# A mixer and mixture-of-experts block: gates applied where expert rows leave PSUM, and another division of the last sums

## The reference, cut to what matters

```python
h2 = rms_norm(x, norm2_g[layer]) * (1 + sc2) + sh2
f = moe_ffn(tokens, router_w, router_b, moe_w1[layer], moe_w3[layer], moe_w2[layer])
#   in moe_ffn, for each expert e:
#   he = jax.nn.silu(h @ w1[e]) * (h @ w3[e])
#   y = y + gates[:, e:e + 1] * (he @ w2[e])
x = x + g2 * f
return rms_norm(x, final_g)
```

## Time and profile before

| | us |
|---|---|
| median of three runs | 611.53 |
| the profiled execution, whole | 612.55 |
| its span, first to last instruction | 610.8 |
| TensorE busy | 546.6 (89%) |
| VectorE busy | 454.0 (74%) |
| ScalarE busy | 319.2 (52%) |
| GpSimd busy | 120.7 (20%) |

### The profile page before, as it was taken

One profiled execution on the slowest core, in us unless ns is written; L12 is line 12 of the kernel. 1 busy time (PEld: TensorE's weight loads), 2 busy tenths in 40 slices (PEclk: granted clock), 3 DMA queues, 4 the chain that ended last, 5 costly groups with the idle time before them and its releaser, 6 DMA issues.

```text
span 610.8 us, 7418 instructions
## 1 busy us (share of the span) xinstructions
PE 546.6 (89%) x2657; PEld 409.5 (67%) x2657; DVE 454.0 (74%) x580; ACT 319.2 (52%) x392; POOL 120.7 (20%) x123
## 2 busy tenths in 40 slices
PE   2889988999999999966999999999999999999860
PEld 2446843677676788733578788888888887877640
DVE  1358695545586545349779999999999999998687
ACT  4531141345425912254357688667768766767214
POOL 5001915333310600025211111001111101100510
PEclk9799998999999999986999999999999999999985
DMA  8999997268214700167789999999999999997543
GB/s 308 389 372 318 380 329 258 86 200 302 70 69 171 243 35 39 66 246 276 241 303 392 379 392 386 393 391 393 391 391 390 387 387 389 363 390 234 182 162 137
DMA packets 88809, 171.50 MB, mean 281 GB/s; under 512 B 5513, under 2 KB 18509, under 8 KB 88785
## 3 DMA queue, kind: packets, MB, share of 16 engines
q1 hardware_dynamic: 82498, 152.81, 70.1%
q10 hardware_dynamic: 2768, 9.97, 4.0%
q0 software_dynamic: 3520, 8.42, 3.8%
HBM read 158.58 MB, written 16.79 MB: 287 GB/s over the span
## 4 chain that ended last, share of the span: by engine, by line
PE 67%; DMA 14%; DVE 8%; ACT 4%; SPq 3%; issue 3%; POOL 0%; DVEq 0%; ACTq 0%; POOLq 0%
DMA ada<-in_ada_w 9%; PE psum L1195 4%; PE psum L1222 4%; PE psum L1197 4%; PE psum L1196 4%; PE psum L1224 4%; PE psum L1223 4%; PE psum L1207 3%; PE psum L1206 3%; PE psum L1205 3%; PE psum L920 3%; DMA w<-in_moe_w 3%; PE psum L922 3%; PE psum L921 3%; PE psum L1057 2%
## 5 line engine op out<-in xcount | busy, mean ns | idle before, releaser
L2058 DVE TENSOR_TENSOR w_lo<-w,w_hi 128x2048 fp32r<-128x2048 f32 x32 | 73.0, 2285 | 2.6 <-ACT w_hi L1574 2.6
L2047 DVE TENSOR_TENSOR w_lo<-w,w_hi 128x1024 fp32r<-128x1024 f32 (+2 forms) x30 | 68.4, 2282 | 0.0
L1574 ACT CAST w_hi<-w 128x2048 fp32r<-128x2048 f32 x32 | 60.4, 1919 | 10.8 <-DMA w<-in_moe_w 5.4
L1565 ACT CAST w_hi<-w 128x2048 fp32r<-128x2048 f32 x30 | 57.2, 1910 | 14.4 <-PE psum L1207 12.0
L2041 DVE TENSOR_TENSOR w_lo<-w,w_hi_a 128x2048 fp32r<-128x2048 f32 (+1 forms) x30 | 51.6, 1758 | 4.7 <-ACT w_hi_a L1561 4.7
L762 POOL COPY idx<-idx 128x1 int32 x14 | 12.6, 903 | 194.7 <-PE psum L1169 184.2
L1222 PE MATMUL psum<-w_hi,heT_hi 128*128 128x512 f32 x120 | 49.7, 414 | 0.8 <-DVE w_lo L2058 0.8
L1740 DVE SCALAR_TENSOR_TENSOR rows<-ada,cc,rows 128x512 f32<-128x512 f32 x48 | 41.6, 871 | 9.1 <-DMA ada<-in_ada_w 7.6
L1224 PE MATMUL psum<-w_hi,heT_lo 128*128 128x512 f32 x120 | 47.0, 392 | 0.0
L1196 PE MATMUL psum<-w_lo,xgT_hi 128*128 128x512 f32 x120 | 46.7, 389 | 0.0
L1223 PE MATMUL psum<-w_lo,heT_hi 128*128 128x512 f32 x120 | 46.7, 389 | 0.0
(11 more groups left out here) (338 smaller groups left out, 1214.3 us busy)
## 6 DMA issues: line engine op xcount, KB each, us to landing
w<-in_moe_w SPq DMA_DIRECT2D x32, 2048.0 KB, 13.8
w<-in_moe_w SPq DMA_DIRECT2D x32, 1024.0 KB, 13.8
ada<-in_ada_w SPq DMA_DIRECT2D x12, 2048.0 KB, 18.1
win<-in_w_in SPq DMA_DIRECT2D x8, 1024.0 KB, 14.5
expert_rows<-ysb ACTq DMA_DIRECT2D x15, 512.0 KB, 6.3
expert_rows<-zero SPq DMA_DIRECT2D x1, 4608.0 KB, 18.4
wout<-in_w_out SPq DMA_DIRECT2D x4, 1024.0 KB, 5.0
x<-in_x SPq DMA_DIRECT2D x2, 1024.0 KB, 9.6
```

The costliest lines, as they stand in the source:

```text
L1574: act.copy(w2_hi[:, :, hs], w2_sb[b][:, :, hs]).then_inc(w2_hi_ok[half], 1)
L2047: v.tensor_tensor(w3_lo[b][:, ks, :], w3_sb[b][:, ks, :], w3_hi[:, ks, :], ALU.subtract).then_inc(w3_lo_ok, n)
L2058: v.tensor_tensor(w2_lo[b][:, :, hs], w2_sb[b][:, :, hs], w2_hi[:, :, hs], ALU.subtract).then_inc(w2_lo_ok[half], 1)
```

## The change

Gates move to the eviction. The router's gate is worked out before the overflow blocks, set out by slot through the same one-hot product (24 more columns, so that product goes from bf16 with 16 columns to fp32 with 40), copied to `gslot`, and for each block GpSimd copies one column to `gs1[b]`, which `expert_rows` takes as a scalar. The rows in DRAM then carry their gate; the sums at the end are plain additions. A row of the last block is now gathered from a spare block of zeros, for which the DRAM tensor and its zero fill grow by one block. The two gathered rows of tile 3 are no longer added by VectorE: TensorE multiplies them by the identity (plain fp32, two products for each half) into the banks in which the one-hot products accumulate, and waits for the last gather before all of them. For tiles 0 and 1 ScalarE writes x times the reciprocal (after the root of tile 1 and of tile 2), GpSimd multiplies by `final_g`, and SyncE's stores wait for that. `low_hidden` for the last block stands ahead of `add_rows(0)`.

```diff
-            gp.wait_ge(idx_ok, 2)
+            def next_gate(b, s):
+                gp.wait_ge(y1_copied, s - 1)
+                gp.sem_inc(gather_go, 1)
+                gp.tensor_copy(gs1[b][:], gslot[:, bass.ds(s, 1)]).then_inc(gs_ok, 1)
+            gp.wait_ge(idx_ok, 3)
+            for b in range(2):
+                gp.tensor_copy(gs1[b][:], gslot[:, b:b + 1]).then_inc(gs_ok, 1)
...
-            with gp.Fori(1, n_pairs) as i:
+            for b in range(2):
+                gather(b, 2 + b)
+            with gp.Fori(2, n_pairs) as i:
                 for b in range(2):
                     gather(b, i * 2 + b)
+                    next_gate(b, i * 2 + b - 2)
...
+            gp.wait_ge(gain_in, 48)
+            for t in range(2):
+                gp.wait_ge(scale_ok, 4 + t)
+                gp.tensor_tensor(ygat[:, t, 1, :], ygat[:, t, 1, :], fing[:], ALU.mult).then_inc(res_gp, 1)
...
-                    m = pe.matmul(bank[6][:, 0:2 * OVER], hot_slot[:, i, :],
-                                  hot_more[:, i].rearrange("p a b -> p (a b)"), start=(i == 0), stop=(i == 2 * NT - 1))
+                    m = pe.matmul(bank[6][:, 0:2 * OVER + NB], hot_mod[:, i, :], hot_more[:, i, :],
+                                  start=(i == 0), stop=(i == 2 * NT - 1))
...
-            pe.wait_ge(hot_last_ok, 1)
+            pe.wait_ge(hot_ok, 4)
+            pe.wait_ge(gat_in[NT - 1], 32)
             for half in range(2):
                 hs = slice(half * 512, (half + 1) * 512)
                 pe.wait_ge((y0_copied, y1_copied)[half], last + 1)
+                for k in range(2):
+                    pe.matmul(tok_bank(NT - 1, half)[:], ident[:], ygat[:, NT - 1, k, hs], start=(k == 0), stop=False)
...
+            def scaled(t):
+                act.wait_ge(rec_ok, t + 1)
+                act.activation(ygat[:, t, 1, :], x1[:, t, :], ACT.Copy, scale=st2[:, t, 7:8]).then_inc(scale_ok, 1)
...
+                if 1 <= t <= 2:
+                    scaled(t - 1)
...
-                v.tensor_tensor(ysb[b][:, cs_], bank[5 + half], rows[:, G2, cs_], ALU.mult
-                                ).then_inc((y0_copied, y1_copied)[half], 1)
+                v.scalar_tensor_tensor(out=ysb[b][:, cs_], in0=bank[5 + half], scalar=gs1[b][:, 0:1],
+                                       in1=rows[:, G2, cs_], op0=ALU.mult, op1=ALU.mult
+                                       ).then_inc((y0_copied, y1_copied)[half], 1)
...
-                    link(v.scalar_tensor_tensor(out=x1[:, t, :], in0=ygat[:, t, k, :], scalar=gate[:, t, k:k + 1],
-                                                in1=x1[:, t, :], op0=ALU.mult, op1=ALU.add))
+                    link(v.tensor_tensor(x1[:, t, :], ygat[:, t, k, :], x1[:, t, :], ALU.add))
...
             gated(last)
+            low_hidden(1, last)
             add_rows(0)
-            low_hidden(1, last)
+            expert_rows(1, last, final, 0)
             add_rows(1)
-            expert_rows(1, last, final, 0)
             low_last(0)
             expert_rows(1, last, None, 1)
+            add_rows(2)
             low_last(1)
-            add_rows(2)
-            add_last(0, 0)
-            add_last(1, 0)
+            v.wait_ge(gain_in, 48)
+            for t in range(3):
+                add_last(t, 0)
             add_last(0, 1)
             add_last(1, 1)
-            add_last(2, 0)
+            add_last(3, 0)
+            result(0)
             add_last(2, 1)
-            v.wait_ge(gain_in, 32)
-            result(0)
-            add_rows(3)
             result(1)
-            add_last(3, 0)
             add_last(3, 1)
             result(2)
             result(3)
```

More of the change, by code:

```diff
@@ L166, in build @@
         xgT_0 = at("xgT_0", 180 * K1, [P, KD, P])
+        hot_mod = at("hot_mod", 176 * K1, [P, NT * 2, P])
+        hot_more = at("hot_more", 198 * K1, [P, NT * 2, 2 * OVER + NB])
         xn = at("xn", 184 * K1, [P, NT, D])
@@ L192, in build @@
         iota_slot = at("iota_slot", cursor[1], [P, P], BF16)
-        in_last = at("in_last", cursor[1] + 256, [P, NT, 2])
-        gate_last = at("gate_last", cursor[1] + 288, [P, NT, 2])
+        gslot = at("gslot", cursor[1] + 352, [P, NB])
+        gs1 = [at(f"gs1_{b}", cursor[1] + 448 + 32 * b, [P, 1]) for b in range(2)]
         idx_last = at("idx_last", cursor[1] + 320, [P, 1])
@@ L247, in build @@
         wsel = rt("wsel", [P, NT, 2])
+        gate = rt("gate", [P, NT, 2])
+        in_last = rt("in_last", [P, NT, 2])
+        spare = rt("spare", [P, 1])
         den = rt("den", [P, NT, 1])
-        hot_blk = rt("hot_blk", [P, NT * 2, OVER])
+        hot_blk = rt("hot_blk", [P, NT * 2, NB])
         hot_base = rt("hot_base", [P, NT * 2, 2, NE], BF16)
-        hot_more = rt("hot_more", [P, NT * 2, 2, OVER], BF16)
         idx_f = rt("idx_f", [P, NB])
@@ L549, in _ @@
             sp.dma_start(y_dram[(NE - 1) * P:, :].rearrange("(p b) (q n) -> p (b q) n", p=P, n=256),
-                         zero[:].unsqueeze(1).to_broadcast([P, (OVER + 1) * 4, 256])).then_inc(stored, 16)
+                         zero[:].unsqueeze(1).to_broadcast([P, (OVER + 2) * 4, 256])).then_inc(stored, 16)
             for i in range(4):
@@ L629, in _ @@
                     cs_ = slice(half * 512, (half + 1) * 512)
-                    sp.wait_ge(res_ok, 2 * t + half + 1)
+                    sp.wait_ge(*((res_gp, t + 1) if t < 2 else (res_ok, 2 * t + half - 3)))
                     sp.dma_start(out_v[:, t, cs_], ygat[:, t, 1, cs_]).then_inc(stored, 16)
@@ L1296, in _ @@
                 pe.wait_ge((y0_copied, y1_copied)[half], last + 1)
+                for k in range(2):
+                    pe.matmul(tok_bank(NT - 1, half)[:], ident[:], ygat[:, NT - 1, k, hs], start=(k == 0), stop=False)
                 pe.wait_ge(ylast_hi_ok, half + 1)
                 for t in range(NT):
-                    pe.matmul(tok_bank(t, half)[:], last_hot[:, t * P:(t + 1) * P], y_hi[:, hs], start=True, stop=False)
+                    pe.matmul(tok_bank(t, half)[:], last_hot[:, t * P:(t + 1) * P], y_hi[:, hs],
+                              start=(t < NT - 1), stop=False)
                 pe.wait_ge(ylast_lo_ok, half + 1)
@@ L1729, in _ @@
             m.then_inc(hc_ok, 1)
[L1731 removed]
+            v.wait_ge(gain_in, 16)
             def mod_row(n):
@@ L2014, in overflow_blocks @@
                                        op0=ALU.mult, op1=ALU.add).then_inc(rmod_ok, 1)
+                pick(wsel[:], prob[:].unsqueeze(2).to_broadcast(E2))
+                link(v.tensor_tensor(den[:], wsel[:, :, 0:1], wsel[:, :, 1:2], ALU.add))
+                link(v.reciprocal(den[:], den[:]))
+                link(v.tensor_tensor(gate[:], wsel[:], wide(den[:], [P, NT, 2]), ALU.mult))
                 above(cs[:, 0, 8:], bank[7][:, NT * NE:(NT + 1) * NE], [P + 1, 2 * P + 1, 3 * P + 1])
@@ L2029, in overflow_blocks @@
                 link(v.tensor_tensor(blk_no[:], blk_no[:], off2[:], ALU.add))
-                fb = [P, NT * 2, OVER]
-                link(v.tensor_tensor(hot_blk[:], iota_blk[:, NE:NB].unsqueeze(1).to_broadcast(fb),
+                fb = [P, NT * 2, NB]
+                link(v.tensor_tensor(hot_blk[:], iota_blk[:].unsqueeze(1).to_broadcast(fb),
                                      blk_no[:].rearrange("p t k -> p (t k)").unsqueeze(2).to_broadcast(fb), ALU.is_equal))
-                v.tensor_scalar(hot_more[:, :, 0, :], hot_blk[:], tok[:, 0:1], None, ALU.mult)
-                v.tensor_tensor(hot_more[:, :, 1, :], hot_blk[:], tok_chunk[:].unsqueeze(2).to_broadcast(fb), ALU.mult
+                v.tensor_scalar(hot_more[:, :, 0:OVER], hot_blk[:, :, NE:], tok[:, 0:1], None, ALU.mult)
+                v.tensor_tensor(hot_more[:, :, OVER:2 * OVER], hot_blk[:, :, NE:],
+                                tok_chunk[:].unsqueeze(2).to_broadcast([P, NT * 2, OVER]), ALU.mult)
+                v.tensor_tensor(hot_more[:, :, 2 * OVER:], hot_blk[:],
+                                gate[:].rearrange("p t k -> p (t k)").unsqueeze(2).to_broadcast(fb), ALU.mult
                                 ).then_inc(hot_ok, 1)
@@ L2104, in overflow_list @@
                 v.tensor_scalar(blk_last[:], more[:], 2.0, float(NE - 1), ALU.mult, ALU.add)
+                v.tensor_scalar(spare[:], more[:], -2.0, float(NB - NE + 1), ALU.mult, ALU.add)
                 link(v.tensor_copy(ovf[:, 8:9], more[0:1, :]))
@@ L2110, in combine_terms @@
                 link(v.tensor_scalar(in_last[:], blk_no[:], blk_last[:, 0:1], None, ALU.is_equal))
-                link(v.tensor_tensor(blk_first[:], in_last[:], blk_no[:], ALU.mult))
-                link(v.tensor_tensor(blk_first[:], blk_no[:], blk_first[:], ALU.subtract))
+                link(v.scalar_tensor_tensor(out=blk_first[:], in0=in_last[:], scalar=spare[:, 0:1], in1=blk_no[:],
+                                            op0=ALU.mult, op1=ALU.add))
                 link(v.scalar_tensor_tensor(out=slot[:], in0=blk_first[:], scalar=float(P), in1=rmod[:],
@@ L2127, in _ @@
             overflow_list()
```

(4 more changed lines are left out.)

33 lines of the change are left out of this document (15 added, 18 removed).

## The result

The changed kernel takes 616.42 us (median of six runs, 613.23 to 621.12) against 610.82 for the kernel before on the same chips: 1.0094 of it, interval 1.0049 to 1.0140. Measured again beside other experiments it was 1.0079 (1.0054 to 1.0103), 615.71 against 610.87, which is +4.8 us. The profiled execution took 616.43 us, its span 614.7.

What follows compares the result with a forecast made beforehand. It took the end to be VectorE's, fed by gathers, and the blocks TensorE's. +1.7 at the start, +1.4 to the first whole tile and +1.0 behind it gave +4.1: 615.6 us against the median, range 610.3 to 617.6.

Steps and rivals of the forecast that it cites:

- The start: Index product before the expert blocks: fp32 passes on TensorE's path, 1.9 us less 0.21, +1.7; bounds 0 and 2.3.
- The loop: Expert blocks: longer evictions and GpSimd's gate copies are hidden and cost nothing; evictions 1.6 us in all if not.
- Rival 4: Expert blocks: gate copies too late for evictions, VectorE waits 0.5 us in 16 blocks, adding 8: 623.6 us; chance 0.03.
- To the first whole tile: End, up to the first finished tile: wait for the last gather, then sums at slow clock; tile whole at 596.6, +1.4.
- The last gather: Ahead of the sums at the end: issued at 581.95, takes 5.7 us to land, at 587.65.
- the clock: TensorE idle 4.6 us before the identity products, which then run at the slow clock: +1.6 us; bounds 0 and 2.3.
- From T to the end: From the first whole tile, called T, to the span's end: T + 16.6 against 15.6 before, +1.0; bounds T + 13.1, T + 17.3.
- The stores: After GpSimd's second product at T + 10.75: six stores in tile order land in 5.5 us, plus 0.35 for issue and final wait.
- full clock (1): Identity products at the end: the clock holds, so 1.6 us less, +2.5: 614.0 us; chance 0.18.
- Rival 2: End: GpSimd's product about 1 us, clock holds, end at T + 13.1: 610.5 us, or 608.8 if the loop swallows 1.7; chance 0.20.
- rival 3: End: GpSimd held by both tile 2 halves and add_last, or 2.8 us twice, T + 17.3 to T + 18: 616.7 us; chance 0.14.

Runs made afterwards that it cites:

- after: The changed kernel as first measured, against the kernel before: 616.42 us, ratio 1.0094.
- after_again: The changed kernel once more, without an edit, beside other runs: 615.71 us, 1.0079 of the kernel before.
- old_tail: The changed kernel with the end as before, keeping gates at eviction, the fp32 index product and GpSimd's gate copies: 613.13 us, 1.0027 of the kernel before.
- old_tail_bf: old_tail with the index product in bf16 as before and a constant ramp in place of the gates: 611.30 us, 1.0000 of the kernel before.
- bf_index: The changed kernel with the index product in bf16 with 16 columns and a constant ramp for the gates: 614.94 us, 1.0070 of the kernel before.
- early_low: The kernel before with one edit, low_hidden of the last block ahead of add_rows(0): 609.70 us, 0.9991 of the kernel before.
- filler: The changed kernel with five thrown-away fp32 products on TensorE before the wait for the last gather: 612.99 us, 1.0032 of the kernel before.
- dve_results: The changed kernel with all four results by VectorE, no scaled copies or GpSimd multiplications: 613.53 us, 1.0039 of the kernel before.
- gp_memset: The changed kernel with GpSimd's multiplications of tiles 0 and 1 replaced by three memsets each: 616.39 us, 1.0082 of the kernel before.

## Why the prediction was right, point by point

It forecast +4.1 us, slower, and the change is +4.8 to +5.6 by the medians. The three stretches below add up to +4.8 in the profile of after and to +4.2 in that of after_again, each against the one profile of the kernel before; the 0.6 to 0.8 between them and the medians isn't assigned to any step. The steps, each measured from its own start:

- **The start, +1.7 forecast.** The product costs 1.49 more (1.70 against the 1.9 that 16 x 0.12 gave), and 1.2 of it arrive at the end of the blocks. old_tail less old_tail_bf is 1.8 by medians, bf_index less after_again 0.8. The mechanism was right and the size near; the 0.25 that vanish weren't forecast.
- **The loop, nothing.** Right, by old_tail_bf. Rival 4, late gate copies, didn't occur, though the copies are three times as long as I would have said from the earlier trace rows's median.
- **To the first whole tile, +1.4 forecast, +2.0 to +2.9 measured.** This is where the size was off, and two terms of the sum were too small in the first profile. The last gather took 6.5 us from its issue, where I took the median of 5.7 from the earlier trace rows and the bound of 6.0. It varies from profile to profile: in after_again, the same kernel, it took 5.6. The eleven profiles of changed kernels have landings from 5.5 to 6.6, the two of the kernel before and early_low 5.4 to 6.0; whether the change has a part in that isn't shown. And the clock cost 2.5 us, above my bound of 2.3, where I took 1.6; over the five profiles it cost 1.4 to 2.5. I carried over what I had read from the earlier trace rows, 3.1 us at half speed; there it was 3.4 us (1.7 lost, not 1.55), and TensorE had started at full clock and fallen later. Here it had fallen during the longer wait (0.50 already at 587 us), and 5.2 us of the sums ran at half speed. The rest of that step is near: filler's first tile comes 7.5 us behind the start of the sums, 7.35 forecast.
- **From T to the end, +1.0 forecast, +0.7 measured.** The order was right as well as the sum. VectorE's first half of tile 2 goes ahead of GpSimd's second product and ends at T + 8.2 (8.35 forecast), the product ends at T + 10.4 (10.75 forecast), because it was held for 0.42 us and not for the 0.75 of a whole half. VectorE's second half comes behind it, at T + 11.0, and the last result ends at T + 12.5. The stores pile up as forecast and land in up to 3.0 us instead of 2.0, the end is 5.9 us behind GpSimd, 5.85 forecast.

The rivals: full clock (1) is refuted by the windows and was made to happen by filler, at 613.0 us; I had 614.0 for it. Rival 2 had the right question, whether GpSimd's second product is over by T + 8.9, and it isn't. Its end at T + 13.1, with the scaled copies on ScalarE and neither GpSimd nor the queue late, wasn't reached in any run: dve_results ends at T + 12.8, but it has no scaled copies, so that closeness confirms nothing. The division of rival 3, both halves of tile 2 ahead of GpSimd's second product, is refuted by the five profiles, in which one half goes ahead. Its number, 616.7, is nearer to the first measurement (616.42) than my 615.6, and that is luck; the second measurement (615.71) is at mine. The forecast's closeness is in part luck too: the start and the last stretch came out 0.5 and 0.3 us under it, and the stretch to T up to 1.5 over it.

What a point forecast of this change could not see is its scatter: six runs of it lie between 613.2 and 621.1. Five of the profiles here have the gather wait with nothing in it, and their "he to T" is 20.0 to 21.4 us, by when the last gather was issued, how long it took and where in the sums the clock came back. A further 1.7 us can come from a slow clock in the first block, as in gp_memset's profile. For the run of 621 there is no profile, and what made it so long stays open.

## What to carry to other kernels

Work moved onto an idle engine is paid for by what it waits for: the two matrix sums were cheap (1.3 us each at full clock), the wait placed ahead of all eight banks was not, and moving it behind those that don't need it gave back the whole loss. Before a bound engine hands an elementwise operation over, add up what the other engine's version takes (2.35 against 1.4 us here), and whether both read SBUF at the same time; then the bound engine waits for the slow one instead of being relieved by it. And look at each part of a change alone: here one part gained 1.5 us in its profile, and the others hid it.

## What the runs showed of the hardware

- Plain fp32 products with few columns: 16 passes of 40 columns took 1.70 us, 0.106 each, no more than the 0.12 of two-column ones, against 0.43 for 512 columns. The bf16 version of eight products takes 0.21 us.
- After 4.5 to 5 us without work TensorE was at 1.2 GHz instead of 2.4 for 2.9 to 5.2 us of the work that followed, and with products thrown away in between at 2.4 throughout.
- A GpSimd copy of a single column (128x1) took 2.8 us beside VectorE's operations of 128x3072 with two SBUF inputs, 0.18 with VectorE idle. Two GpSimd products of 128x1024 and two VectorE operations of 0.75 us that read two SBUF operands took turns, one of each at a time, so that VectorE's two lasted 4.2 us; memsets of 128x1024, three in a row, held VectorE not at all (1.42 us).
- Indirect gathers of 128 rows, eight in a row, took 5.4 to 6.6 us from issue to landing over the thirteen profiles; six stores of 256 KB issued together landed in 2.0 to 3.0 us each.
